# Second mixer of a two-block transformer kernel: attention by head pairs, and attention and long convolution placed between the weight tiles of hyena inputs and gates

## The reference, cut to what matters

```
q, k, v, hv, hx1, hx2, gna, ghy = split(h @ w_in)        # h: 256 x 1024, w_in: 1024 x 5120
k_c, v_c = split(ctx_modulated @ w_in[:, 512:1536])       # 256 context tokens
# neighbourhood attention, 8 heads of 64
s = concat(rope(q) rope(k)^T * scale + bias(mask), q k_c^T * scale)   # 256 x 512 per head
y_na = softmax(s) @ concat(v, v_c)
# hyena: short convolution of 3 taps, then two gated long convolutions by Fourier transform
u = short_conv(concat(hv, hx1, hx2)); z = u[0]
for n in 0, 1: z = u[n + 1] * long_conv(z, filter[n])
y_hy = z
m = sigmoid(gna) * (y_na @ w_na_o) + sigmoid(ghy) * (y_hy @ w_hy_o)
x = x + g1 * (m @ w_out)
```

## Time and profile before

| | |
|---|---|
| time, median of 3 runs | 1084.31 us (1081.74 to 1087.27) |
| profiled execution | 1087.21 us, of which its span is 1085.4 us |
| granted TensorE clock, mean | 0.979 |
| TensorE matmuls busy | 94% of the span |
| VectorE, ScalarE, GpSimd busy | 73%, 46%, 15% |

### The profile page before, as it was taken

One profiled execution on the slowest core, in us unless ns is written; L12 is line 12 of the kernel. 1 busy time (PEld: TensorE's weight loads), 2 busy tenths in 40 slices (PEclk: granted clock), 3 DMA queues, 4 the chain that ended last, 5 costly groups with the idle time before them and its releaser, 6 DMA issues.

```text
span 1085.4 us, 20702 instructions
## 1 busy us (share of the span) xinstructions
PE 1024.9 (94%) x7714; PEld 955.6 (88%) x7714; DVE 793.4 (73%) x1302; ACT 497.6 (46%) x751; POOL 165.2 (15%) x173
## 2 busy tenths in 40 slices
PE   6679999999999988999999999999998999999996
PEld 3279999999988888999999988998557999999996
DVE  5979888788766677999777736754665878976554
ACT  3155444344545444445444423576343465554441
POOL 2650000011000047000045102000221150000011
PEclk9789999999999999999999999999899999999998
DMA  6247777667633324657445333552012447754452
GB/s 222 78 155 255 268 264 257 211 233 254 210 118 135 137 88 185 231 210 265 164 169 201 136 117 117 194 185 97 25 30 83 154 177 280 262 179 159 160 186 90
DMA packets 38105, 188.32 MB, mean 174 GB/s; under 512 B 4423, under 2 KB 8296, under 8 KB 24936
## 3 DMA queue, kind: packets, MB, share of 16 engines
q1 hardware_dynamic: 38056, 187.66, 48.8%
HBM read 186.60 MB, written 1.05 MB: 173 GB/s over the span
## 4 chain that ended last, share of the span: by engine, by line
PE 77%; DVE 13%; ACT 3%; issue 3%; DMA 2%; SPq 1%; DVEq 0%; ACTq 0%; POOL 0%
PE ps L386 23%; PE ps L388 22%; PE ps L387 22%; DVE wl L334 4%; PE ps L1919 1%; DMA sini<-in_sini 1%; ACT wh L328 1%; PE ps L1932 1%; PE ps L1705 1%; DVE xl L1200 1%; DVE dump L1220 1%; DMA stage<-in_w_k 1%; PE ps L1898 1%; DVE dump L1226 1%; PE ps L1909 1%
## 5 line engine op out<-in xcount | busy, mean ns | idle before, releaser
L386 PE MATMUL ps<-xh,wh 128*128 128x256 f32 (+3 forms) x1808 | 522.6, 289 | 15.0 <-DVE xl L1200 8.5
L388 PE MATMUL ps<-xl,wh 128*128 128x256 f32 (+3 forms) x1808 | 519.6, 287 | 0.0
L387 PE MATMUL ps<-xh,wl 128*128 128x256 f32 (+3 forms) x1808 | 518.4, 287 | 0.0
L334 DVE TENSOR_TENSOR wl<-stage,wh 128x1024 fp32r<-128x1024 f32 (+2 forms) x320 | 366.6, 1156 | 130.0 <-ACT wh L328 127.6
L328 ACT ACTIVATE wh<-stage 128x1024 fp32r<-128x1024 f32 (+2 forms) x320 | 307.1, 969 | 214.4 <-PE ps L388 177.9
L386 PEld LDWEIGHTS ps<-xh,wh 128*128 128x128 f32 x1808 | 343.9, 190 | 20.1 <-DVE xl L1200 9.9
L387 PEld LDWEIGHTS ps<-xh,wl 128*128 128x128 f32 x1808 | 344.5, 191 | 1.8 <-issue 0.2
L388 PEld LDWEIGHTS ps<-xl,wh 128*128 128x128 f32 x1808 | 343.2, 190 | 1.4
L386 PE MATMUL ps<-gh,wh 128*128 128x256 f32 (+1 forms) x528 | 150.1, 284 | 2.9 <-DVE wl L334 1.5
L387 PE MATMUL ps<-gh,wl 128*128 128x256 f32 (+1 forms) x528 | 149.4, 283 | 0.0
L388 PE MATMUL ps<-gl,wh 128*128 128x256 f32 (+1 forms) x528 | 148.9, 282 | 0.0
(11 more groups left out here) (245 smaller groups left out, 870.0 us busy)
## 6 DMA issues: line engine op xcount, KB each, us to landing
stage<-in_w_gu SPq DMA_DIRECT2D x66, 1024.0 KB, 4.8
stage<-in_w_dn SPq DMA_DIRECT2D x48, 704.0 KB, 4.1
adaw<-in_w_ada SPq DMA_DIRECT2D x48, 512.0 KB, 5.2
stage<-in_w_gates SPq DMA_DIRECT2D x8, 1024.0 KB, 4.8
stage<-in_w_hy SPq DMA_DIRECT2D x6, 1024.0 KB, 4.7
stage<-in_w_q SPq DMA_DIRECT2D x8, 512.0 KB, 4.7
stage<-in_w_k SPq DMA_DIRECT2D x8, 512.0 KB, 4.8
stage<-in_w_v SPq DMA_DIRECT2D x8, 512.0 KB, 5.2
```

The costliest lines, as they stand in the source:

```text
L334: nc.vector.tensor_tensor(wl[:, b, w], stage[:, b, w], wh[:, b, w].bitcast(fp32), ALU.subtract).then_inc(split_lo, 1)
L386: nc.tensor.matmul(psum, wh[:, b, w], xhi, start=first and n == 0, stop=False)
L387: nc.tensor.matmul(psum, wl[:, b, w], xhi, start=False, stop=False)
L388: last = nc.tensor.matmul(psum, wh[:, b, w], xlo, start=False, stop=close and n == len(blocks) - 1)
```

## The change

It touches the second mixer alone. The number of weight tiles and their matmuls stay the same.

- Stage 2 is dissolved: the four swaps of k stand behind the four v tiles, the transposes of v behind the q tiles, the swaps of q behind the first two mixer tiles. VectorE's scaling of the residual `h` (8 instructions) moves from behind `hy` to between the v tiles.
- `hy` and `gates` become one row of 28 mixer tiles written out without loops, on three banks of PSUM in turn (`n % 3`). Tile n may start when tile n-3 has been read. Behind the tiles stand, at fixed places, the units of attention and the parts of the convolution. For unit u the score is behind tile 3u+2, the transposes behind 3u+4, the product with v behind 3u+5; spectra behind tiles 9, 10, 18, 19; inverse transforms behind 13, 15 and 22 to 25; the hyena transposes behind 5 and 8.
- There are 8 units, each for two heads and one half of the queries. The matmuls of the two heads alternate, as in the first block. The bias is added in place in PSUM for both heads, one reduction over 128 x 2 x 512 gives both maxima, the exponentials read PSUM directly. One unit is in flight; its banks are 3 and 4 for scores and transposes, 5 for the result.
- A gate tile is only copied out (`gate_copy`); two sigmoids of 128 x 2048 follow after the last tile (`gates_closed`), and VectorE's first gate product waits for both.
- ScalarE makes the high part of tile n+4 and VectorE its low part within their work for tile n, behind what the list below shows.
- `mix` rotates over banks 1 to 4, begins with its hyena half, and finds its first four tiles split already; its input lies in the other half of `xh`/`xl` (`ALT`).
- SyncE loads the bias of two heads at a time, between the chunks.

```diff
+HY_TILES = 2 * NCHUNK["hy"]
+MIXER_TILES = HY_TILES + 2 * NCHUNK["gates"]
+NA_UNITS = NA_HEADS
+def unit_scored(n):
+    return (n - 2) // 3 if n % 3 == 2 and n < 2 + 3 * NA_UNITS else None
+def unit_turned(n):
+    return (n - 4) // 3 if n % 3 == 1 and 4 <= n < 4 + 3 * NA_UNITS else None
+def unit_attended(n):
+    return (n - 5) // 3 if n % 3 == 2 and 5 <= n < 5 + 3 * NA_UNITS else None
...
@@ SyncE
+            for d in range(MIXER_TILES // 2):
+                s = "hy" if d < NCHUNK["hy"] else "gates"
+                load_chunk(s, PAIR0["hy"] + d // 2, d % 2)
+                for u in range(2, NA_UNITS):
+                    if d == (3 * u + 5) // 2:
+                        sp.wait_ge(bias_used, u - 1)
+                        load_bias(u)
...
@@ ScalarE
+            def na_exponentials(u):
+                act.wait_ge(na_max, u + 1)
+                if u:
+                    act.wait_ge(na_turned, u)
+                for h2 in range(2):
+                    ins = act.activation(pr[:, h2, :], ps[3 + h2][:, :], ACT.Exp, bias=nst[:, 0, h2:h2 + 1],
+                                         accum_out=nst[:, 0, 2 + h2:3 + h2])
+                ins.then_inc(na_exp, 1)
+            def na_turned_back(u):
+                act.wait_ge(na_turned, u + 1)
+                if u:
+                    act.wait_ge(na_av, u)
+                act.activation(prt[:, :, :], banks[:, 3:5, :], ACT.Copy).then_inc(na_prt, 1)
+            def gates_closed(m0, m1):
+                act.wait_ge(gate_read, 2 * m1)
+                act.activation(gates[:, m0:m1, :, :], gates[:, m0:m1, :, :], ACT.Sigmoid).then_inc(gates_ready, 1)
+            for n in range(MIXER_TILES):
+                tile_landed(n)
+                if n < HY_TILES:
+                    conv_centre(n)
+                else:
+                    gate_copy(n)
+                if unit_turned(n) is not None:
+                    na_turned_back(unit_turned(n))
+                hi_part(*four_ahead("hy", n))
+                if unit_attended(n) is not None and unit_attended(n) % 2:
+                    na_out_hi(unit_attended(n) // 2)
+                if n in (5, 8):
+                    for j in range(2):
+                        hyena_tokens(2 * (n // 8) + j)
+                if n in (9, 10, 18, 19):
+                    for part in range(2):
+                        spectrum_back((9, 10, 18, 19).index(n), part)
+                if unit_scored(n) is not None:
+                    na_exponentials(unit_scored(n))
+                if n in (24, 26):
+                    for m in range(2):
+                        hyena_out_hi(n - 24 + m)
+            for m in range(2):
+                gates_closed(4 * m, 4 * m + 4)
...
@@ VectorE
+            def na_front(u):
+                dve.wait_ge(na_scored, u + 1)
+                dve.wait_ge(bias_in[u % 2], 32 * (u // 2 + 1))
+                both = banks[:, 3:5, 0:TX]
+                dve.tensor_tensor(both, both, bias[:, u % 2, :, :], ALU.add).then_inc(bias_used, 1)
+                dve.wait_ge(bias_used, u + 1)
+                dve.reduce_max(nst[:, 0, 0:2], banks[:, 3:5, :], AX.X, negate=True).then_inc(na_max, 1)
+            def na_back(u):
+                dve.wait_ge(na_exp, u + 1)
+                link(dve.reciprocal(nst[:, 0, 4:6], nst[:, 0, 2:4]))
+                for h2 in range(2):
+                    ins = dve.tensor_scalar(pr[:, h2, :], pr[:, h2, :], nst[:, 0, 4 + h2:5 + h2], None, ALU.mult)
+                ins.then_inc(na_prob, 1)
+            for n in range(MIXER_TILES):
+                if n and unit_scored(n - 1) is not None:
+                    na_back(unit_scored(n - 1))
+                if n < HY_TILES:
+                    conv_sides(n)
+                if n < 2:
+                    for i in range(2):
+                        rope_back(KN + 2 * n + i)
+                if unit_scored(n) is not None:
+                    na_front(unit_scored(n))
+                lo_part(*four_ahead("hy", n))
+                if unit_attended(n) is not None and unit_attended(n) % 2:
+                    na_out_lo(unit_attended(n) // 2)
+                if n in (10, 11, 19, 20):
+                    spectrum_product((10, 11, 19, 20).index(n))
+                if n == 15:
+                    for t in range(2):
+                        second_signal(t)
+                if n in (23, 25):
+                    for m in range(2):
+                        hyena_out(n - 23 + m)
+                if n in (25, 27):
+                    for m in range(2):
+                        hyena_out_lo(n - 25 + m)
...
+            dve.wait_ge(gates_ready, 2)
...
@@ TensorE
+            for n in range(MIXER_TILES):
+                mixer_tile(n)
+                if n < 2:
+                    for i in range(2):
+                        swap_halves(KN + 2 * n + i)
+                if unit_turned(n) is not None:
+                    na_turn(unit_turned(n))
+                if unit_attended(n) is not None:
+                    na_attend(unit_attended(n))
+                if unit_scored(n) is not None:
+                    na_score(unit_scored(n))
+                if n in (5, 8):
+                    for j in range(2):
+                        turn_hyena(2 * (n // 8) + j)
+                if n in (9, 10, 18, 19):
+                    for part in range(2):
+                        spectrum((9, 10, 18, 19).index(n), part)
...
+            def na_score(u):
+                for query, lo in ((q2r, 0), (q2, TX)):
+                    for h2 in range(2):
+                        o = HD * h2
+                        ins = pe.matmul(ps[3 + h2][:, lo:lo + TX], query[o:o + HD, p, t * P:(t + 1) * P],
+                                        kxc[o:o + HD, p, lo:lo + TX], start=True, stop=True)
+                ins.then_inc(na_scored, 1)
+            def na_attend(u):
+                for i in range(4):
+                    for h2 in range(2):
+                        o, c = HD * h2, P * p + HD * h2
+                        ins = pe.matmul(ps[5][o:o + HD, t * P:(t + 1) * P], vtok[:, i, c:c + HD],
+                                        prt[:, h2, i * P:(i + 1) * P], start=i == 0, stop=i == 3)
+                ins.then_inc(na_av, 1)
```

More of the change, by code:

```diff
@@ L54 @@
 QKV_PAIRS = NCHUNK["qkv"] // 2
-WAITED_FOR = ("q2", "gates", "mix", "out")
+WAITED_FOR = ("out",)
 HALVES = {16: (8, 8), 11: (6, 5), 8: (4, 4)}
@@ L630, in _, with load_bias @@
             sp.dma_start(swap[:, :], A["swap"]).then_inc(mixer_const_in, 16)
-            for u in range(2):
[L632 to L643, removed]
+            def load_bias(u):
+                for h2 in range(2):
+                    row = (2 * (2 * (u // 2) + h2) + u % 2) * P
+                    sp.dma_start(bias[:, u % 2, h2, :], A["bias"][row:row + P, :]).then_inc(bias_in[u % 2], 16)
+            chunks("v2")
+            for u in range(2):
+                load_bias(u)
+            chunks("q2")
+            for d in range(MIXER_TILES // 2):
[4 more added lines that the diff above has]
+                        sp.wait_ge(bias_used, u - 1)
+                        load_bias(u)
+            chunks("mix")
             chunks("out")
@@ L964, in _ @@
             root("final1", TX)
[L966 to L991, removed]
@@ L992, in _ @@
-            through(act, "gates", sigmoids, hi_part)
-            for j in range(4):
+            for s in ("k2", "v2"):
+                for n in range(4):
+                    hi_part(*four_ahead(s, n))
+            for n in range(4):
+                hi_part(*four_ahead("q2", n))
+                act.wait_ge(v2_turned, n + 1)
+                act.activation(vtok[:, :, n * P:(n + 1) * P], ps[4 + n][:, :].rearrange("p (t d) -> p t d", t=4),
+                               ACT.Copy).then_inc(v2_tok, 1)
@@ L1030, in hyena_out_hi @@
                 act.wait_ge(yh_ready, m + 1)
[L1031 to L1046, removed]
-                elif u == 14:
-                    hyena_out_hi(0)
-                    hyena_out_hi(1)
-                elif u == 15:
-                    hyena_out_hi(2)
@@ L1068, in _ @@
-            through(act, "mix", merge_hi, hi_part)
-            late_splits("mix", hi_part)
-            through(act, "out", o_hi_next("out", "norm2", TX), hi_part)
+            for m in range(KD):
+                if m < KD - 2:
+                    hi_part(*four_ahead("mix", m))
+                act.wait_ge(merged, m + 1)
+                act.activation(xh[:, m, 0:TX], ms[:, m % 2, :], ACT.Copy).then_inc(merged_hi, 1)
+            for m in range(KD - 2, KD):
+                hi_part(*four_ahead("mix", m))
@@ L1658, in _ @@
+            for m in range(KD - 2, KD):
+                lo_part(*four_ahead("mix", m))
+            wide_residual("out", TX, "norm2", lambda m: mods[:, ds(G1 + m, 1)], ALT)
             dve.wait_ge(prod_re, 4)
```

429 lines of the change are left out of this document (191 added, 238 removed).

## The result

The changed kernel takes 1052.91 us (median of 4 runs, 1050.56 to 1054.60) against 1085.71 of the kernel before on the same chip (1081.74 to 1087.27). The ratio is 0.9702, 95% interval 0.9667 to 0.9736: 32.4 us less, between 28.7 and 36.2. The forecast was 22 less, 1062.3 at the median; the direction was right and the time lies just inside the lower end of the range (1052), but the gain came out half as large again. That the time lies inside the range, by 0.9 us, is luck: single executions fall on both sides of 1052. Of the cases that the prediction named it is nearest the third rival, fewer waits; that rival had the clock stay up as well, and in the profiled execution it did not.

A forecast was written before the change was run, and what follows sets the result against it. TensorE bounds the kernel; ideal gain 95.8 - 63.1 = 32.7 us, less 9.6 of new waits and 1.7 of low clock, 21.4, taken as 22 for overlapping waits: 1084.3 - 22 = 1062.3 us, range 1052 to 1074.

The forecast's parts named there:

- the third rival: Fewer waits: a `spectrum_product` costs 2.1 to 2.3 us and the clock stays up; 5 to 7 us return, 1056; chance 0.12.
- The bound: Whole kernel: TensorE, busy 94% of the span; 95.8 us of the second mixer, besides its tiles, can shrink.
- TensorE's pieces: Mixer work besides tiles: swaps 3.6, transposes of v and hyena 4.2, spectra and inverse transforms 28.7, eight attention units 26.6; 63.1 us.
- New waits of units 0, 3 and 6: Attention units: VectorE's other work delays them, 1.4 us for unit 0, 2.7 for unit 3, 3.0 for unit 6.
- The first `mix` tile: Start of `mix`: TensorE waits 2.5 us for the last two hyena inputs, written behind the low part of tile 31.
- The clock: Mixer: one low-clock stretch of half the earlier 6.81 us, 3.4 us at half speed, costs 1.7; bounds 0 and 6.8.
- Sigmoids covered by under 1 us: Gates to first `out` tile: ScalarE's late sigmoids cost nothing, hidden by under 1 us; every further microsecond of delay shows.
- rival 1: Attention: the two heads do not overlap, so the 15.0 us stay away; gain 7, 1077; chance 0.06.
- 2 falls: Attention: the unit's chain is too long in every unit; 1.5 us show in each of 8, 12 in all, 1074; chance 0.14.
- 5 with both: Attention: heads do not overlap and the chain is too long in every unit; nothing to tell, near 1084; chance 0.03.
- 4 falls: Mixer tiles: weight parts come late, queued behind waiting units; at 1 us a tile 6 us slower, 1090; chance 0.04.
- three signs of failure: Mixer: transposes wait in every unit, tiles wait for L334, or `out` starts by waiting for L1653's successor.

## Why the gain was larger than predicted, step by step

**The bound.** Right. The time came out of TensorE's idle time and its poorly used instructions in one stretch, and TensorE is the bound there still.

**TensorE's pieces**, 63.1 us. Nearly right: 57.11 + 137.87 - 1.2 of waits are 193.8, less the 54.0 that TensorE was busy on k, v and q tiles before and 28 x 2.83 of mixer tiles leaves 60.5. Pairs of heads cost 1.06 and 1.03 (predicted 1.10 and 1.16), eight transposes 0.79 between the starts instead of twice 0.53. Changing between the whole array and its halves cost little: a product starts 0.20 us behind the last matmul of a tile (683.34 to 683.54), where the matmuls of a tile start 0.12 apart. The worth of the pairs, 15.0, was shown by keeping the heads apart (14.5). That the chain is covered by tiles was shown by taking the tiles away; its slack was 0.9 us and not 0.5. What the smaller parts of the change are worth, such as the later sigmoids and the order of `mix`, no run tells apart.

**New waits of units 0, 3 and 6**, 7.1 us: this is the step that failed, by its size. It measured 1.2. The price "0.69 + 2 x 1.64 = 4.0" for a `spectrum_product` came from the earlier trace rows, where VectorE's and GpSimd's halves start together. In the changed kernel GpSimd begins its half of the second product when the spectra are there (713.44), while VectorE still has its half of the first, and is through (718.09) before VectorE gets to it (720.73): 2.1 us, the lower bound that the prediction had written down and not taken; its third rival named this case. With GpSimd made to overlap, the price was 4.1 and the waits were 3.6 and 3.7, above the 2.7 and 3.0 of the prediction, whose sum had left out that the low part stretches too. Unit 0's 1.4 was a guess between 0 and 3 and came out 0.

**The first `mix` tile**, 2.5 us: right, 2.3, by the queue that was named; moving two instructions took it away.

**The clock**, 1.7: right for the profiled execution, in which 3.4 us at 0.51 follow that wait, but by luck: that one stretch would be left, of half the length of 6.81, was a guess. And 6.81 was not all that the kernel before had in its attention: the mean clock of 0.94 over 83.99 us asks for some 10, and there was a second stretch.

```profile
820.40:823.80 3.40, 3.40 (x13) 2.80 (x13) 1.70 (x7) 2.07 (x8) 0.00 (x0) 0.50 0.91 344
```

In the changed kernel it does not come in every profile: of the eight profiles with the same wait of 2.3 us, four have a low stretch behind it (the changed kernel twice, heads apart, GpSimd longer) and four have none.

**Sigmoids covered by under 1 us**: right that they are covered, wrong in the working. The 5.71 us between the two rows were taken for two merges without a wait, but VectorE was busy for only 5.17 of them and had waited for TensorE in between; without waits it is 5.07, so it catches up some 0.6 us every two tiles and the cover was thicker than said.

**The sum.** Up to the first `mix` tile the forecast was 32.7 - 7.1 = 25.6, measured 34.6: 5.9 from the waits, 2.6 from the pieces, 0.5 from the idle time just before 661.04, which the stretch had left out. Behind it 4.2 was forecast and 3.8 measured, and the forecast of 22 had taken 0.6 more than its terms give (21.4), for waits that overlap. The last 1.9 us of the difference of the two profiled executions lie in code that is the same in both. 1.3 of them stand ahead of the k tiles, where the low stretches fell differently: the granted clock was 0.79 before and 1.00 after from 292 to 300 us, 0.86 and 0.72 from 404 to 416. No run shows a cause in the change.

Of the rivals, the overlap was there (rival 1 falls), the chain fitted in every unit but two (2 falls, and 5 with both), late weight parts never stopped a tile (4 falls). Of the signs, the score pair's 1.06 and the product's 1.03 us, the 2.3 us in the first `mix` tile and the units without idle time came as written; units 3 and 6 waited less, and `mix` began 35.9 us earlier instead of 22. None of the three signs of failure came.

## What to carry to other kernels

When a price depends on what another engine does at that moment, price it at the time when both will stand there, not by the rows in which they happened to meet. A distance between two starts is a cost only if there is no wait inside it. And a chain through several engines (here TensorE, VectorE, ScalarE and back) can be placed at a fixed distance in tiles of the bounding engine: its length can be worked out from rows beforehand, and came out here within half a microsecond (5.1 forecast, 4.7 measured).

## What the runs showed of the hardware that was not expected

- Two groups of fp32 matmuls on different halves of the array run side by side even when the program has one group wholly behind the other: for scores (groups of 2 matmuls) at no loss, for products with v (groups of 4) in 1.51 us against 1.03 in alternation and 2.04 kept apart.
- The length of a wait of TensorE did not tell whether the low clock followed. The waits of 3.6 and 3.7 us with GpSimd longer were each followed by 3.4 us at 0.50 or 0.51, and one of 3.22 us with the transposes a tile earlier by 3.4 us at 0.53; one of 3.65 us in that same profile was not (1.00). The wait of 2.3 us was in four of eight profiles. No wait of 2.04 us or less was, in the profiles that have the units between the tiles; in the kernel before, 2.20 us in its attention was the earlier trace rows.
- VectorE's tensor_tensor of 128 x 1024 over two SBUF inputs took 2.33 us beside GpSimd and 1.22 alone.
